# Attention masks added by VectorE in the operation that takes the maximum, and five other edits to a tuned fp32 layer

## What is computed

```python
mod_x = silu_c @ w_mod + b_mod                 # shifts, scales, gates: 6 rows of 1024
hx = rms_norm(x, norm1_w) * (1 + sc1) + sh1
hc = rms_norm(ctx, norm1_w) * (1 + csc1) + csh1
rx, rgx, qx, kx, vx, gax, gbx = split_cols(hx @ w_in)
rc, _, _, kc, vc, _, _ = split_cols(hc @ w_in)
y_rx = rglru_output(...)                       # conv of 4 taps, two gates, scan both ways over ctx + x
q, k = apply_rope(qx), apply_rope(kx)
# blocks of 128 queries; keys: previous, own and next block, and 256 context keys
s_loc = where(|kpos - qpos| <= 128, q @ k_neighbours.T / sqrt(128), -1e30)
s_ctx = q @ kc.T / sqrt(128)
m = max(s_loc.max, s_ctx.max, sink); p = exp(s - m)
y_ax = (p_loc @ v_neighbours + p_ctx @ vc) / (p_loc.sum + p_ctx.sum + exp(sink - m))
x = x + g1 * ((sigmoid(gax) * (y_rx @ w_o_rnn) + sigmoid(gbx) * (y_ax @ w_o_attn)) @ w_out)
x = x + g2 * conv_ffn(rms_norm(x) * (1 + sc2) + sh2)
return rms_norm(x, final_norm_w)
```

## Time and profile before

| what | before |
|---|---|
| runs | 1876.41, 1877.39 and 1885.78 us, median 1877.39 |
| profiled execution | 1886.7 us, span 1884.9 us |
| mean granted TensorE clock | 0.976 of full speed |
| busy: TensorE, VectorE, ScalarE, GpSimd | 1777.4, 1228.9, 714.8, 597.7 us |

### The profile page before, as it was taken

How to read it: one execution, slowest core, us unless ns; L and a number is a source line. 1 busy time by engine, 2 the same in 40 slices (tenths; PEclk the granted TensorE clock), 3 DMA queues, 4 the chain that set the end, 5 groups by cost and what they waited for, 6 DMA issues and landing times.

```text
span 1884.9 us, 22989 instructions
## 1 busy us (share of the span) xinstructions
PE 1777.4 (94%) x8276; PEld 1467.2 (78%) x8276; DVE 1228.9 (65%) x1355; ACT 714.8 (38%) x919; POOL 597.7 (32%) x276
## 2 busy tenths in 40 slices
PE   3998899999899969999999899999999999999997
PEld 1887688888688767878887676888888888888886
DVE  5873667767513677775214969999999998525423
ACT  5433666556200157772002014444444444302212
POOL 2115777676344645543443870000000000000000
PEclk8999899999899979999999899999999999999999
DMA  9123111111145300005122750222222223522212
GB/s 384 33 89 123 42 48 64 62 48 55 68 156 167 89 12 1 0 1 190 67 89 83 307 200 23 101 90 78 89 80 87 78 89 133 218 101 91 94 45 90
DMA packets 52941, 182.11 MB, mean 97 GB/s; under 512 B 10512, under 2 KB 10896, under 8 KB 50704
## 3 DMA queue, kind: packets, MB, share of 16 engines
q1 hardware_dynamic: 45200, 148.26, 22.2%
q10 hardware_dynamic: 7680, 33.04, 5.0%
HBM read 145.09 MB, written 30.93 MB: 93 GB/s over the span
## 4 chain that ended last, share of the span: by engine, by line
PE 70%; DVE 17%; issue 4%; ACT 3%; DMA 3%; POOL 2%; ACTq 1%; SPq 0%; DVEq 0%; POOLq 0%
PE acc L838 14%; PE acc L839 14%; PE acc L840 14%; PE gp L838 9%; PE gp L840 9%; PE gp L839 9%; DVE pt_lo L2093 2%; DVE smax L2063 2%; DVE wgr L2129 2%; DMA qs<-qf 1%; DVE yq L2046 1%; PE acc L873 1%; DVE qs L2043 1%; ACTq L1509 1%; DMA wgr<-in_mod_rest 1%
## 5 line engine op out<-in xcount | busy, mean ns | idle before, releaser
L838 PE MATMUL acc<-hx_hi,whi_both 128*128 128x512 f32 x672 | 266.0, 396 | 32.0 <-DVE hx_lo L1864 17.6
L839 PE MATMUL acc<-hx_lo,whi_both 128*128 128x512 f32 x672 | 264.8, 394 | 0.0
L840 PE MATMUL acc<-hx_hi,wlo_both 128*128 128x512 f32 x672 | 264.1, 393 | 0.0
L683 POOL TENSOR_TENSOR whi_both<-wst,ones 128x1024 fp32r<-128x1024 f32 x63 | 172.8, 2743 | 270.0 <-PE acc L840 202.0
L685 POOL TENSOR_TENSOR wlo_both<-wst,whi_both 128x1024 fp32r<-128x1024 f32 x63 | 189.9, 3014 | 4.9
L838 PEld LDWEIGHTS acc<-hx_hi,whi_both 128*128 128x128 f32 x672 | 128.3, 191 | 61.4 <-DVE hx_lo L1864 18.5
L840 PEld LDWEIGHTS acc<-hx_hi,wlo_both 128*128 128x128 f32 x672 | 128.1, 191 | 27.2
L839 PEld LDWEIGHTS acc<-hx_lo,whi_both 128*128 128x128 f32 x672 | 128.2, 191 | 25.9
L838 PE MATMUL acc<-T_hi,fac_hi 128*128 128x512 f32 x264 | 102.8, 389 | 0.3 <-DVE fac_lo L2287 0.3
L840 PE MATMUL acc<-T_hi,fac_lo 128*128 128x512 f32 x264 | 102.7, 389 | 0.0
L839 PE MATMUL acc<-T_lo,fac_hi 128*128 128x512 f32 x264 | 102.7, 389 | 0.0
(11 more groups left out here) (335 smaller groups left out, 4790.6 us busy)
## 6 DMA issues: line engine op xcount, KB each, us to landing
wst<-in_w_in SPq DMA_DIRECT2D x50, 512.0 KB, 3.4
wst<-in_w_up SPq DMA_DIRECT2D x26, 512.0 KB, 3.9
wgr<-in_mod_rest ACTq DMA_DIRECT2D x6, 2048.0 KB, 10.8
ffn_row_scratch<-ca SPq DMA_DIRECT2D x24, 512.0 KB, 2.6
wst<-in_w_down SPq DMA_DIRECT2D x32, 384.0 KB, 3.1
g_in<-ffn_row_scratch SPq DMA_DIRECT2D x24, 512.0 KB, 6.8
wup<-in_w_up SPq DMA_DIRECT2D x22, 512.0 KB, 4.1
wmod<-in_mod_first SPq DMA_DIRECT2D x8, 1024.0 KB, 19.2
```

The costliest lines, as they stand in the source:

```text
L683: nc.gpsimd.tensor_tensor(whi[s][:, 0:kc, :], wst[s][:, 0:kc, :], ones_of(kc), mult).then_inc(S["w_hi"], 1)
L838: mm(out_ap, w_h, x_h, start=first, stop=False)
L839: mm(out_ap, w_h, x_l, start=False, stop=False)
L840: return mm(out_ap, w_l, x_h, start=False, stop=last)
```

## The change

Six edits:

1. Start: VectorE adds the squares in pairs (`pair_squares`), so TensorE sums four chunks, not eight. `scaled` multiplies by both factors in one operation, ScalarE only adds the shift while it makes the high part, `low_x` adds the shift itself. `low_x` of chunk k-1 stands between the two L1850 of chunk k. The modulation is loaded in twice as many DMAs. The low parts of the two value blocks are made by VectorE, not GpSimd.
2. Context rows: a context row is made inside the recurrence from the weight block that is there anyway (`context_row`); seven weight loads and splits go, and so does `xc_ctx`. The row's 256 columns share a bank with the merge gate.
3. Queries: `qf` and `qs` are double, the swaps have a semaphore each; the split of the keys comes before the queries, not near their end.
4. Attention: the masks stand in `window`, 5 blocks of 128 in bf16 (mask before, zero, mask after, zero, zero). One VectorE operation per head adds scores and window, multiplies by -scale, writes the result to `prob` and takes the minimum with the negated sink. The mask matmuls and L2066 go. The exponential works in place on `prob`. TensorE may overwrite the scores after this operation, not after the exponential. The last query block uses two operations.
5. GpSimd splits the first two weight blocks of the merge in four parts in units 1, 2, 3 and 15, not in unit 0.
6. Output product: the weight blocks and the residual rows are loaded earlier, the 2 MB groups by SyncE's queue; the first `add_group` stands before the second read, not before the first.

```diff
-W_S1, W_S2, W_Q, W_S4, W_S5, W_S6 = 10, 32, 42, 50, 66, 74
+W_S1, W_S2, W_Q, W_S4, W_S5, W_S6 = 5, 25, 35, 43, 59, 67
...
 # TensorE
-            for c in range(KC):
-                weights(W_RC + c)
...
+            def context_row(c, n):
                 for k in range(KC):
-                    last = three(rc_bank(c), whi[n][:, k, :], wlo[n][:, k, :], hc_hi[:, k, :], hc_lo[:, k, :], k == 0, k == KC - 1)
+                    last = three(rc_bank, whi[n % 2][:, k, :], wlo[n % 2][:, k, :], hc_hi[:, k, :], hc_lo[:, k, :], k == 0, k == KC - 1)
                 last.then_inc(S["rc_full"], 1)
...
             def chunk_step(i, e, j):
+                if not later(i, 2):
+                    first_step()
+                    return
...
                 half(A_S1, n_r, 0, hx_hi, hx_lo)
                 gate(i - 1, 1)
+                pe.wait_ge(S["rc_read"], i)
+                if later(i, 3):
+                    pe.wait_ge(S["ga_read"], 2 * i - 4)
+                context_row(i, n_r)
                 half(A_S1, n_r, 1, hx_hi, hx_lo).then_inc(S["acc_full"], 1)
                 gate(i - 1, 2)
+                weights(n_ga, 6, j)
+                pe.wait_ge(S["rc_read"], i + 1)
+                merge_gate_half(i, n_ga, 0)
...
-                    pe.wait_ge(S["s_exp"], 4 * u + h - 1)
+                    pe.wait_ge(S["s_neg"], 4 * u + h - 1)
...
-                for e in range(2):
-                    if not is_edge(n) or (n == 0) == (e == 1):
-                        m0 = 384 if e else o0
-                        mm(pair[:, m0:m0 + P], ident_b[:, :], masks_b[:, e, :], start=False, stop=False)
 # ScalarE
-                    if not (isinstance(i, int) and i == 0 and s == 0):
-                        act.wait_ge(S["q_rope"], 2 * i + s)
+                    if not (isinstance(i, int) and i == 0):
+                        act.wait_ge(S["q_rope"], 2 * i + s - 1)
...
-                act_of(prob[kh][:, h, P if edge else 0:], gp[:, c0:1024 * (h % 2) + 768], ACT.Exp, scale=SCALE,
-                       bias=negm[:, kh, h:h + 1], accum_out=rsum[:, kh, h:h + 1]).then_inc(S["s_exp"], 1)
+                row = prob[kh][:, h, P if is_edge(n) else 0:]
+                act_of(row, row, ACT.Exp, scale=-1.0, bias=negm[:, kh, h:h + 1], accum_out=rsum[:, kh, h:h + 1])\
 # VectorE
+            def pair_squares(j):
+                dve.wait_ge(S["sq_done"], 2 * j + 2)
+                v.tensor_tensor(xsq[:, 2 * j + 1, :], xsq[:, 2 * j + 1, :], xsq[:, 2 * j, :], add).then_inc(S["sq_pair"], 1)
...
+            def masked(n, kh, h, cols, mask, bound, result):
...
+                return v.tensor_tensor_reduce(prob[kh][:, h, P * first:P * first + cols.stop - cols.start], pair[:, cols],
+                                              window[:, mask:mask + (cols.stop - cols.start) // P, :].rearrange("p b n -> p (b n)"),
+                                              -SCALE, bound, add, ALU.min, result)
...
-                v.reduce_max(smax[:, kh, h:h + 1], pair[:, lo:768], AX.X).then_inc(S["s_max"], 1)
...
-                v.tensor_scalar(negm[:, kh, h:h + 1], smax[:, kh, h:h + 1], -SCALE, nsink[:, hd:hd + 1], mult, ALU.min)\
...
-            row_product(1)
             for m in range(KC):
-                if m < 6:
-                    add_group(m + 2)
+                if m == 1:
+                    row_product(1)
+                if 1 <= m < 7:
+                    add_group(m + 1)
 # SyncE
+            for m in range(3):
+                load_out(m)
+            sp.wait_ge(S["merged"], KC)
+            load_xres(0, 0)
+            load_xres(1, 1)
+            full(sp, A_S4 + 15)
+            load_groups(2)
+            load_out(3)
+            load_groups(3)
+            for m in range(2, KC):
+                slot_read(sp, A_S5 + m - 2)
                 load_xres(m, m % 2)
+                load_out(m + 2)
+                store_x1(m - 2)
+                if m < 6:
+                    load_groups(m + 2)
```

More of the change, by code:

```diff
@@ L869, in _ @@
             pe.wait_ge(S["consts_set"], 2)
-            for k in range(KC):
-                pe.wait_ge(S["sq_done"], k + 1)
+            for k in range(KC // 2):
+                pe.wait_ge(S["sq_pair"], k + 1)
                 for h in range(2):
-                    last = mm(acc[0][:, HALF * h:HALF * (h + 1)], ones[:, :], xsq[:, k, HALF * h:HALF * (h + 1)],
-                              start=k == 0, stop=k == KC - 1)
+                    last = mm(acc[0][:, HALF * h:HALF * (h + 1)], ones[:, :], xsq[:, 2 * k + 1, HALF * h:HALF * (h + 1)],
+                              start=k == 0, stop=k == KC // 2 - 1)
             last.then_inc(S["acc_full"], 1)
@@ L969, in merge_gate_half, with first_step @@
                 last.then_inc(S["ga_full"], 1)
+            def first_step():
+                weights(W_S1)
+                slot_free(A_S1 + 2)
+                half(A_S1 + 2, W_S1, 0, hx_hi, hx_lo)
+                gate(0, 0)
+                pe.wait_ge(S["rc_read"], 1)
+                context_row(1, W_S1)
+                gate(0, 1)
+                half(A_S1 + 2, W_S1, 1, hx_hi, hx_lo).then_inc(S["acc_full"], 1)
+                gate(0, 2)
+                weights(W_S1 + 1)
+                slot_free(A_S1 + 3)
+                half(A_S1 + 3, W_S1 + 1, 0, hx_hi, hx_lo)
+                gate(0, 3)
+                half(A_S1 + 3, W_S1 + 1, 1, hx_hi, hx_lo).then_inc(S["acc_full"], 1)
             def chunk_step(i, e, j):
-                n_r, n_ga, n_rg = (w_chunk(e, q) for q in range(3)) if later(i, 2) else (W_S1 + 2, None, W_S1 + 3)
-                per = 6 if later(i, 2) else 0
+                if not later(i, 2):
+                    first_step()
+                    return
+                n_r, n_ga, n_rg = (w_chunk(e, q) for q in range(3))
                 gate(i - 1, 0)
-                weights(n_r, per, j)
+                weights(n_r, 6, j)
                 slot_free(A_S1, 2, i)
@@ L1619, in _ @@
             reload_row(1)
-            for g in range(2, 5):
-                load_groups(g)
             row_again(1)
@@ L1849, in modulation @@
                         dve.wait_ge(S["mod_sum"], n + j)
[L1850 removed]
+                    v.scalar_tensor_tensor(out=junk[:, :], in0=wmod[k][j][:, :], scalar=1.0, in1=silu[e][:, :], op0=mult, op1=mult,
                                            accum_out=msum[:, e, j, k:k + 1]).then_inc(S["mod_sum"], 1)
+                    if j == 0 and between is not None:
+                        low_x(between)
                 dve.wait_ge(S["mod_sum"], n + 2)
@@ L1879, in _ @@
             for k in range(1, KC):
-                modulation(k, 0)
+                modulation(k, 0, between=k - 1)
                 scaled(k)
-                low_x(k - 1)
-            low_x(KC - 1)
             dve.wait_ge(S["silu_ready"], 2)
-            for k in range(3):
+            modulation(0, 1, between=KC - 1)
+            modulation(1, 1)
+            for n in range(W_V, W_RC):
+                dve.wait_ge(S["w_hi"], n + 1)
+                v.tensor_tensor(wlo[n % 2][:, :, :], wst[n % 2][:, :, :], whi[n % 2][:, :, :], sub).then_inc(S["w_ready"], 1)
+            for k in range(2, 5):
                 modulation(k, 1)
```

330 lines of the change are left out of this document (159 added, 171 removed).

## The result

The changed kernel took 1851.32, 1855.96, 1856.34 and 1855.14 us, median 1855.55, the kernel before beside it 1877.1. The ratio is 0.987 with a 95% interval of 0.984 to 0.990; a second round of five runs gave 1855.41 and 0.987 (0.986 to 0.989). So the edits are worth 22 to 23 us, where the forecast said 35 from the median: 1842, with a range of its own of 1834 to 1850 and an outer range of 1830 to 1858. The time is inside the outer range and 5.5 us outside the forecast's own. The first profiled execution took 1851.3 us against 1886.7 before, 35.4 less, where the sum said 36.8. The sum fits the two profiled executions and not the median. That fit is in part luck: the one before was among the kernel's longest executions, and the one after was the shortest of nine. This is what the experiments are about.

What follows compares the result with a forecast made beforehand. TensorE was taken as the bound, busy 1777.4 of 1884.9 us, so gains were matmuls removed or gaps closed. The terms sum to 36.8; from median 1877.39 that gives 1840.6, stated as 1842, own range 1834 to 1850, outer 1830 to 1858.

Steps and rivals of the forecast that it cites:

- Taking the sum from the median: Whole kernel: the summed gain subtracted from median 1877.39, not from the profiled 1886.7, giving 1840.6, stated as 1842 us.
- the sum of 36.8: Whole kernel: gains of 5.5 start, 7.4 context rows, 10.4 queries, 5 attention and 8.5 output product, in us.
- Start: Ones-products fed by pairs end 2.8 us earlier and the first low part comes 2.75 earlier: 5.5 us gained.
- Context rows: Recurrence's beginning, 133.5 to 204.5 us: six rows move into later chunks, 71.0 becomes 63.6, gain 7.4 (bounds 5 and 10).
- 2 of a possible 0 to 3: Recurrence's beginning: us that TensorE waits for the first gate, behind VectorE's taps, cast and low part.
- near 174: Recurrence: sign to look for, start in us of the second chunk's first half, 204.51 before.
- The rival of a wait in each chunk: Recurrence: merge gate waits for VectorE's taps behind slowed scans, 1 to 2 us in six chunks: 1851, chance 0.08.
- Queries: Last query head: its copy comes when the product ends, not after earlier rotations; gain 10.4 us (bounds 9 and 12).
- Attention: Masked operation of 0.93 us replaces mask matmuls, maximum and bound: 0.35 us per unit, 5 us over some 14 units.
- The rivals with a dear operation: Attention: masked operation takes 1.1 to 1.5 us, giving 1852 to 1878, chance 0.13; half rate or worse, some 1890, chance 0.03.
- Output product: The 8.76 us wait for the second weight block goes, then VectorE is next: gain 8.5 us (bounds 4 and 11.6).
- The lock that I had weighed for the masked operation: Attention: VectorE-GpSimd port lock, taken not to hold the masked operation; if general, the sum up to 10 us smaller.

Runs made afterwards that it cites:

- before_new_output: The kernel before with the output product's edit alone: ten runs at 1870.7 to 1872.7 us, two at 1880.2 and 1882.3.
- before_new_queries: The kernel before with the queries' edit alone (two buffers each, keys split ahead): median 1877.8 us.
- rep_after: The changed kernel profiled a second time, nothing edited: 1856.38 us.
- gates_early_hold: The changed kernel with GpSimd's first-chunk order changed: next weights and gates split earlier, first branch gate's weight split held for VectorE's low part; median 1849.0 us.
- gates_and_low: gates_early_hold with the split of the second output block held until VectorE has made the merge's last low part: median 1845.7 us.
- two_masked: The changed kernel with each head's masked operation cut in two (384 and 256 columns) in the twelve units not at an edge: median 1871.6 us.

## Why the prediction was right, and where it was off

*Taking the sum from the median* is the step that failed most. The sum was made from a profiled execution on the kernel's upper level and then subtracted from the median, which is the lower level. I wrote that "some of the gaps may be shorter" and allowed 1.4 us for it. It was one gap, the queries', and 7.2 us. In a usual execution the last copy comes 164.3 us behind the recurrence's end, with two buffers 163.3 (traces of before_new_output and before_new_queries): there was 1 us to gain on that path and not 10.4. Of the 14.5 us by which the sum of 36.8 was too high, 7 are the queries', 5 the context rows', and nearly 3 those of the output product with the merge in front of it; start and attention nearly cancel. What set the level was in the trace of before and I did not ask for it: each head's copy waited for the previous sum though TensorE's product had ended before, and that sum took 3.2 us instead of 1.2.

*Start*: 5.5 forecast, 4.75 between the first profiles (39.81 against "near 39"), 4.8 by undoing it. Right; the missing 0.8 are the four ones-products, which took 8.7 us and not 8.0 and ended 2.0 earlier, not 2.8.

*Context rows*: 7.4 forecast, 6.6 between the first profiles, 3.7 between the middles of all traces (449.43 in five with the old recurrence, 445.77 in seven with the new). The mechanism was right, six rows moved and the tail of 3.9 and 2.3 to 2.6 kept. Mis-sized is the first gate's wait, "2 of a possible 0 to 3": it is 3.0 in four of seven traces, and there the clock goes down behind it, which I had not charged. So the second chunk's first half came at 176.90, and at 180.35 in rep_after, for the "near 174" of the forecast. Without these waits the kernel is 6.4 us faster by the medians (gates_early_hold), and the stage 4.3 us shorter than the middle of the seven, 6.1 in the trace of gates_and_low. The rival of a wait in each chunk did not come; TensorE has no wait between 177 and 480 us.

*Queries*: 10.4 forecast and 11.5 between the profiles, both reckoned from a long execution before. On the usual one the stage gained 3.5 to 4.3, of which 1.9 to 2.7 are the attention edit's and 1 to 2 those of the two buffers (by doing and undoing it). The keys' split ahead of the queries was hidden, as said.

*Attention*: 5 forecast, 5.9 to 6.6 in its stage, and 8.1 by undoing it, with the part ahead of the stage. The operation's length was right (879 for 881), but it costs the chain less than taken: 0.80 us from its start to a low part behind it, not 0.93, since the read-out overlaps. The unit period is 10.23 for the forecast 10.4. The rivals with a dear operation are out, by these rows and by two_masked, which shows what they would have cost.

*Output product*: 8.5 forecast. The stage gained 9.0 and the merge in front lost 3.1, 5.9 net; by undoing and by doing it 5.3 and 5.1. The split of the second block, which I put "beside" the merge as hidden, stands beside VectorE's last low parts. The lock that I had weighed for the masked operation I did not think of here. In the output product VectorE is next, as said: its reads are 11.4 to 13.4 us apart, four rows of the modulation and one read.

By stages from usual executions (before_new_output up to the merge, against rep_after; for the merge and behind it the kernel before, whose 181.0 and 103.7 the usual execution of before_new_queries has too) the gains are 4.8, 2.2, 3.5, 5.9, -3.1 and 8.9 us, 22.3 in all, and the medians say 22 to 23: nothing of size is left over. What stays open is what sends an execution of the kernel before to the upper level. A late head was shown to be enough, and in the traces the level goes with whether the first head's sum starts ahead of GpSimd's split or behind it. Both hang on transfers (the swapped rows, the weight block), and which of them decides in one execution of five is not shown.

## What to carry to other kernels

Before a sum is taken from a profiled execution, look where that execution stands among the runs; if it is off by more than the runs scatter, find the stage that differs, since an edit that mends that stage gains on some executions only. A loop whose copy waits for its own last result, beside another engine of the same period, can run in two rhythms; a second buffer removes the slow one, and is worth that even if the median doesn't move. And each split that is moved "beside other work" has to be checked against what VectorE does there with two inputs from SBUF: here another order on GpSimd in the recurrence gave 6 us, and one wait that holds a split back in the merge gave 3.

## What the runs showed of the hardware

The kernel before has two levels of time, 8 us apart (16 of 78 runs on the upper one), with no change of the program, and the trace shows both rhythms. A wait of TensorE of 2.1 us was followed by matmuls at the full clock in three traces, one of 3.0 us by a stretch partly at the lower level in four. From the first gate to the next wait 30.3 us passed in the three and 31.8 to 33.1 in the four, so 0.9 us more waiting came with 1.4 to 2.7 us more behind it. The masked operation (sum of scores and a bf16 mask, scaled, minimum taken, fp32 result written) takes 879 ns for 640 columns, 747 for 512, 612 for 384 and 476 to 484 for 256, that is some 1.05 ns a column and 0.21 us fixed.
